# First two layers: mixed tiles turned inside the last input unit, and the gate's Silu split

## What is computed

```python
proj = jnp.einsum('btd,de->bte', x, w_in[l])                 # 2048 -> 7168 columns
ca, cg, hq, hf, hi, hg, rq, rk, rv, rg = jnp.split(proj, split_idx, axis=-1)
y_conv = conv_mixer(ca, cg, ...)                             # 512 columns
y_hgrn = hgrn2_mixer(hq, hf, hi, hg, ...)                    # 768 columns
y_ret = retention_mixer(rq, rk, rv, rg, positions, ...)      # 768 columns
mix = jnp.concatenate([y_conv, y_hgrn, y_ret], axis=-1)
h = jnp.einsum('bte,ed->btd', mix, w_out[l])
x = layer_norm(ALPHA * x + h, ln1_g[l], ln1_b[l])
...                                                          # feed-forward, layer norm
```

```python
o = ((o - mu) * lax.rsqrt(var + LN_EPS)).reshape(b, t, D_RET) * gn_g + gn_b
return jax.nn.silu(g_in) * o                                 # g_in is rg, the last 768 columns of proj
```

## Time and profile before

| | us |
|---|---|
| time, median of 3 runs | 3481.93 (3479.95 to 3484.95) |
| time of the profiled execution | 3486.19 |
| span of the profiled execution, first to last instruction | 3484.4 |
| mean granted TensorE clock | 0.992 of full |

### The profile page before, as it was taken

One profiled execution on the slowest core, in us unless ns is written; L12 is line 12 of the kernel. 1 busy time (PEld: TensorE's weight loads), 2 busy tenths in 40 slices (PEclk: granted clock), 3 DMA queues, 4 the chain that ended last, 5 costly groups with the idle time before them and its releaser, 6 DMA issues.

```text
span 3484.4 us, 42756 instructions
## 1 busy us (share of the span) xinstructions
PE 3397.1 (97%) x15987; PEld 2831.8 (81%) x15987; DVE 2222.3 (64%) x2582; ACT 1586.0 (46%) x1958; POOL 352.4 (10%) x390
## 2 busy tenths in 40 slices
PE   8999999999999999989999999999999989999999
PEld 7788778888888787878788888888888879888877
DVE  6986566555555788855665656666446676655654
ACT  4544444444444446434444434344455643455553
POOL 0034001010101000340101010100000132000100
PEclk9999999999999999999999999999999999999999
DMA  7645566666666664446766676766655601565634
GB/s 238 181 140 163 181 199 219 200 211 200 212 199 212 190 194 151 145 151 193 245 210 208 203 207 203 207 196 208 186 178 176 205 6 56 188 189 169 179 118 163
DMA packets 333659, 633.83 MB, mean 182 GB/s; under 512 B 27545, under 2 KB 37785, under 8 KB 331819
## 3 DMA queue, kind: packets, MB, share of 16 engines
q1 hardware_dynamic: 313104, 595.93, 55.4%
q0 software_dynamic: 11168, 29.18, 2.7%
q10 hardware_dynamic: 9216, 6.30, 0.6%
HBM read 612.44 MB, written 2.10 MB: 176 GB/s over the span
## 4 chain that ended last, share of the span: by engine, by line
PE 85%; DVE 9%; ACT 3%; DMA 1%; POOL 1%; issue 1%; SPq 0%; DVEq 0%; ACTq 0%; POOLq 0%
PE ps_unit L279 26%; PE ps_unit L281 26%; PE ps_unit L280 26%; DVE sb_w_lo L262 3%; DVE sb_conv_y L1260 2%; PE ps_mix L2732 2%; PE ps_mix L1334 1%; DMA sb_raw<-in_w_in_dram 1%; ACT sb_w_hi L255 1%; PE ps_mix L708 0%; PE ps_mix L307 0%; DVE sb_x L438 0%; PE ps_mix L3129 0%; PE ps_mix L3109 0%; DMA sb_raw<-in_e_w_in_dram 0%
## 5 line engine op out<-in xcount | busy, mean ns | idle before, releaser
L262 DVE TENSOR_TENSOR sb_w_lo<-sb_raw,sb_w_hi 128x1024 fp32r<-128x1024 f32 x1120 | 1377.2, 1245 | 1001.4 <-ACT sb_w_hi L255 996.4
L255 ACT ACTIVATE sb_w_hi<-sb_raw 128x1024 fp32r<-128x1024 f32 x1120 | 1172.6, 1059 | 1456.9 <-DMA sb_raw<-in_w_ff_dram 532.3
L279 PE MATMUL ps_unit<-sb_w_hi,sb_a_hi 128*128 128x512 f32 x3456 | 1365.3, 395 | 16.0 <-DVE sb_a_lo L750 11.1
L281 PE MATMUL ps_unit<-sb_w_hi,sb_a_lo 128*128 128x512 f32 x3456 | 1351.6, 391 | 0.0
L280 PE MATMUL ps_unit<-sb_w_lo,sb_a_hi 128*128 128x512 f32 x3456 | 1350.7, 391 | 0.0
L279 PEld LDWEIGHTS ps_unit<-sb_w_hi,sb_a_hi 128*128 128x128 f32 x3456 | 652.8, 189 | 155.2 <-DVE sb_a_lo L750 12.7
L281 PEld LDWEIGHTS ps_unit<-sb_w_hi,sb_a_lo 128*128 128x128 f32 x3456 | 652.0, 189 | 137.6
L280 PEld LDWEIGHTS ps_unit<-sb_w_lo,sb_a_hi 128*128 128x128 f32 x3456 | 653.1, 189 | 132.2
L279 PE MATMUL ps_unit<-sb_w_hi,sb_f_hi 128*128 128x512 f32 x1024 | 399.3, 390 | 0.0
L281 PE MATMUL ps_unit<-sb_w_hi,sb_f_lo 128*128 128x512 f32 x1024 | 398.6, 389 | 0.0
L280 PE MATMUL ps_unit<-sb_w_lo,sb_f_hi 128*128 128x512 f32 x1024 | 398.5, 389 | 0.0
(11 more groups left out here) (463 smaller groups left out, 1975.6 us busy)
## 6 DMA issues: line engine op xcount, KB each, us to landing
sb_raw<-in_w_ff_dram SPq DMA_DIRECT2D x512, 512.0 KB, 3.8
sb_raw<-in_w_in_dram SPq DMA_DIRECT2D x224, 512.0 KB, 3.6
...
```

The source lines that it names most:

```text
L255: k.nc.scalar.activation(k.w_hi[:, j], k.raw[:, j], ACT.Copy).then_inc(k.hi_ready, 1)
L262: k.nc.vector.tensor_tensor(k.w_lo[:, j], k.raw[:, j], k.w_hi[:, j].bitcast(F32), ALU.subtract).then_inc(k.lo_ready, 1)
L279: k.nc.tensor.matmul(acc, hi[:, kt, tokens], w_hi, start=kt == 0, stop=False)
L281: last = k.nc.tensor.matmul(acc, lo[:, kt, tokens], w_hi, start=False, stop=kt == KT - 1)
```

## The change

It moves the turning of all eight banks in each of the two layers, four of them into the last input unit.

- Retention's output stands ahead of block 89 in layer 0 and of block 91 in layer 1 (`RET_OUT`).
- Banks 0, 1 and 2 are transposed right behind it, and bank 3 ahead of block 92 (layer 0) or 94 (layer 1). ScalarE's rounding of them waits for the block of the last input unit that still reads that part of `a_hi`. Banks 1 and 2 lie in half 0 of `ps_unit`, banks 0, 3 and 4 in bank 3 of `ps`, and banks 5, 6 and 7 in banks 0 to 2 of `ps`.
- Bank 4 is turned ahead of block 2 of the out product, and 5, 6 and 7 ahead of block 4.
- `turn_source`'s first 5 are raised at the start of `dve_retention`.
- The gate's Silu goes in two: the first 256 columns in `proj` during the last unit, the other 512 straight from the sums in `ps_unit`, in the place of the last unit's copy. VectorE's gate products wait for that and stand ahead of its last three weight blocks.

```diff
 def pe_out_units(pe, k, mixed, tile):
     first = k.block0["pe"]
     k.block0["pe"] += OUT_UNITS * BLOCKS
-    pe_turn_start(pe, k, mixed)
     for c in range((OUT_UNITS - 1) * BLOCKS):
-        if c < BLOCKS:
-            pe_turn_step(pe, k, mixed, c)
+        if c == 0:
+            pe.wait_ge(*k.turn_lo.next("pe", 3))
+        if c == 2:
+            pe.wait_ge(*k.turn_lo.next("pe bank", 3))
+            pe_mixed_bank(pe, k, mixed, 4)
+        if c == 4:
+            for g in (5, 6, 7):
+                pe_mixed_bank(pe, k, mixed, g)
+        if 3 <= c < BLOCKS:
+            pe.wait_ge(*k.turn_lo.next("pe"))
         pe_block(pe, k, first, c, k.a_hi, k.a_lo)
+def mixed_bank(k, g):
+    return k.ps_unit[:, 0, g - 1, :] if g in (1, 2) else k.ps[:, 3 if g in (0, 3, 4) else g - 5, :]
+def pe_mixed_bank(pe, k, mixed, g):
+    pe.wait_ge(*k.turn_source.next("pe"))
+    pe_turn_bank(pe, k, mixed, g, mixed_bank(k, g))
+def act_mixed_bank(act, k, run, g):
+    act.wait_ge(k.block_done, run.first + run.blocks + g + 1)
+    act_turn_bank(act, k, g, mixed_bank(k, g))
...
 # pe_retention
-    upto(run, 88 + LATE * l)
+    upto(run, RET_OUT[l])
...
     last.then_inc(*k.r_o.up())
+    for g in (0, 1, 2):
+        pe_mixed_bank(pe, k, first_mix_tile(k), g)
+    upto(run, RET_OUT[l] + 3)
+    pe.wait_ge(*k.turn_lo.next("pe bank"))
+    pe_mixed_bank(pe, k, first_mix_tile(k), 3)
     run.rest()
+RET_OUT = (89, 91)
 # act_retention
-    upto(run, 91 + LATE * l)
+    upto(run, RET_OUT[l] + 1)
+    for g in (0, 1, 2):
+        act_mixed_bank(act, k, run, g)
     act.wait_ge(*k.r_var.next("act"))
     a.activation(k.r_rstd[:], k.r_mv[:, :, 1], ACT.Sqrt, ...)
+    run(1)
+    act.wait_ge(*run.evacuated(run.blocks // BLOCKS - 1))
+    rg = k.proj[:, :, RG:RG_LAST]
+    a.activation(rg, rg, ACT.Silu).then_inc(*k.r_gate.up())
+    upto(run, RET_OUT[l] + 4)
+    act_mixed_bank(act, k, run, 3)
     run.rest()
-    rg = k.proj[:, :, RG:RG + HW]
-    act.wait_ge(*run.evacuated(run.blocks // BLOCKS))
-    a.activation(rg, rg, ACT.Silu).then_inc(*k.r_gate.up())
+def act_take_first(act, k):
+    take_proj = act_take_proj(act, k, HQ)
+    def take(b0, s, i):
+        if HQ + (2 * i + s) * NC < RG_LAST:
+            return take_proj(b0, s, i)
+        wait_unit(act, k, b0, s)
+        k.nc.scalar.activation(k.proj[:, :, RG_LAST:RG_LAST + NC], k.ps_unit[:, s], ACT.Silu).then_inc(k.evacuated, BLOCKS)
+    return take
 # dve_retention: turn_source moved to its start; then, behind the statistics of o
-    upto(run, 92 + LATE * l)
+    for g in (0, 1, 2):
+        dve_turn_bank(dve, k, g, mixed_bank(k, g))
+    run(1)
...
-    upto(run, 94 + LATE * l)
+    run(1)
+    dve_turn_bank(dve, k, 3, mixed_bank(k, 3))
     step(v.tensor_tensor(y, y, k.r_shift[:]..., ALU.add))
-    run.rest()
     dve.wait_ge(*k.r_gate.next("dve"))
+    dve.wait_ge(*run.evacuated(run.blocks // BLOCKS))
     for p in range(HEADS // 2):
         v.tensor_tensor(y, y, gate, ALU.mult).then_inc(*k.turn_source.up())
+    run.rest()
+    dve_turn_bank(dve, k, 4, mixed_bank(k, 4))
...
-                act_out_units(act, k, act_ln_root(act, k))
+                act_out_units(act, k, act_ln_root(act, k), late={AHEAD + 1: (4,), AHEAD + 3: (5, 6, 7)})
-                dve_out_units(dve, k, LayerNorm(ALPHA))
+                dve_out_units(dve, k, LayerNorm(ALPHA), late={AHEAD + 2: (5, 6, 7)})
```

More of the change, by code:

```diff
@@ L497, in pe_out_units @@
     k.block0["pe"] += OUT_UNITS * BLOCKS
-    pe_turn_start(pe, k, mixed)
     for c in range((OUT_UNITS - 1) * BLOCKS):
-        if c < BLOCKS:
-            pe_turn_step(pe, k, mixed, c)
+        if c == 0:
[8 more added lines that the diff above has]
+            pe.wait_ge(*k.turn_lo.next("pe"))
         pe_block(pe, k, first, c, k.a_hi, k.a_lo)
+    k.turn_lo.next("pe bank", 4)
     pe_seam_last(pe, k, first, OUT_UNITS - 1, k.a_hi, k.a_lo, tile)
@@ L536, in pe_pair_after_seam, with act_out_units @@
         pe_block(pe, k, first, c, k.a_hi, k.a_lo)
-def act_out_units(act, k, root):
+def mixed_bank(k, g):
[6 more added lines that the diff above has]
+    act_turn_bank(act, k, g, mixed_bank(k, g))
+def act_out_units(act, k, root, late={}):
     first = k.block0["act"]
@@ L543, in act_out_units, with dve_out_units @@
         act_split(act, k, first, c)
+        for g in late.get(c, ()):
+            act_turn_bank(act, k, g, mixed_bank(k, g))
     act_seam(act, k, first, OUT_UNITS * BLOCKS, root)
-def dve_out_units(dve, k, norm):
+def dve_out_units(dve, k, norm, late={}):
     first = k.block0["dve"]
@@ L555, in dve_out_units @@
             dve_split(dve, k, first, u * BLOCKS + c)
+            for g in late.get(u * BLOCKS + c, ()):
+                dve_turn_bank(dve, k, g, mixed_bank(k, g))
     last = OUT_UNITS - 1
@@ L1036 @@
 RQ, RK, RV, RG = (2 * CONV_C + (4 + n) * HW for n in range(4))
+RG_LAST = RG + HW - NC
 LEVELS = 7
@@ L1683, in dve_retention @@
     v.memset(k.r_rstd[:], 0.0).then_inc(*k.r_rope_free.up())
+    dve.wait_ge(*k.conv_done.next("dve"))
+    dve.sem_inc(*k.turn_source.up(BLOCKS - HEADS // 2))
     upto(run, 85 + LATE * l)
@@ L1692, in dve_retention @@
             .then_inc(*k.r_kept.up())
-    upto(run, 89 + LATE * l)
+    upto(run, RET_OUT[l] + 1)
     dve.wait_ge(*k.r_o.next("dve"))
@@ L1706, in dve_retention @@
     for t in range(TT):
+        if t:
+            run(1)
         for h in range(HEADS):
@@ L1711, in dve_retention @@
     step(last)
-    dve.wait_ge(*k.conv_done.next("dve"))
-    dve.sem_inc(*k.turn_source.up(BLOCKS - HEADS // 2))
     y = k.proj[:, :, RQ:RQ + HW]
     step(v.tensor_tensor(y, y, k.r_gain[:].unsqueeze(1).to_broadcast([P, TT, HW]), ALU.mult))
-    upto(run, 94 + LATE * l)
+    run(1)
+    dve_turn_bank(dve, k, 3, mixed_bank(k, 3))
     step(v.tensor_tensor(y, y, k.r_shift[:].unsqueeze(1).to_broadcast([P, TT, HW]), ALU.add))
-    run.rest()
     dve.wait_ge(*k.r_gate.next("dve"))
+    dve.wait_ge(*run.evacuated(run.blocks // BLOCKS))
     for p in range(HEADS // 2):
```

5 lines of the change are left out of this document (2 added, 3 removed).

## The result

The changed kernel takes 3463.43 us (median of 5 runs, 3457.69 to 3465.19), the kernel before beside it 3479.95 us (median of 5). The ratio is 0.9944 with the interval [0.9933, 0.9956]: 19.5 us of 3481.93, between 15.3 and 23.3. The forecast was 3464.4 us, between 3460.5 and 3471.5. The profiled execution took 3463.43 us with a span of 3461.6.

The account below looks back on a forecast made before the run. TensorE, busy 97% of the span, was taken as the bound, so time comes only from its waits and slow clock. 7.60 plus 10.48 us removed, 18.1, less 0.6 added gave 17.5: 3481.93 to 3464.4 us, range 3460.5 to 3471.5.

Parts of the forecast that it names:

- All the waits named: TensorE idle to be removed: 4.75 and 1.26 us in layer 0, 4.97 and 2.50 us in layer 1.
- the new one of 0.6 us: Layer 1: the output, one block earlier, waits 0.6 us for the last masked score; the clock was assumed to stay.
- The three terms: Layer 0: 4.75 us idle before the out product, 1.59 slow block behind it, 1.26 ahead of retention's output; together 7.60.
- the removed part: Layer 1, 10.48 us: idle 4.97 and 2.50, slow transposes 1.76, slow block behind them 1.25.
- the term left out of the sum: Layer 1: slow clock in the next four transposes, 0.97 us against 0.60, kept only for the low end.
- weight block 99: Layer 0: its low part, behind the gate products, ready at 385.5 and needed at 389.9, 4.4 us to spare.
- 1.6 us, from one row, for any new stall: Slow clock behind any new wait, taken from layer 0's block of 4.44 us in place of 2.85.
- The prediction's own use of the rule, 5.5 us: Both layers: half of 4.0, 3.7 and some 3.3 us as throttling penalty, 5.5 us where the rows give 4.6.
- A new stall: Rival: bank 5's round or weight block 99 late, 7.2 us come back, gain 10.3, 3471.6 us; chance 0.13.
- the weights: Rival: TensorE reaches the out product sooner but waits for weights, gain about 4 us, 3478; chance 0.04.
- the late load: Rival: weight block 101 lands late, delaying gate products and weight block 99; 7 us slower, 3489; chance 0.03.
- The fall of the clock: Rival: clock falls anyway with 12 transposes behind retention's output, 1.6 us per layer, gain 14.3, 3467.6 us; chance 0.08.

Follow-up runs that it names:

- e12_out88: Changed kernel with retention's output at its old places in both layers, behind block 87 in layer 0 and 91 in layer 1: 3459.00 us, ratio 0.9940.
- e9_out92: Changed kernel with layer 1's retention output moved one block later: 3459.31 us, ratio 0.9943.
- The dose: Changed kernel with eight extra ScalarE copies ahead of the Silu on the sums in layers 0 and 1: 3471.11 us, ratio 0.9977.
- e1 to e4: Change in layer 0 only, 0.9974; layer 1 only, 0.9972; kernel before with Silu's split only, 0.9986; changed kernel, banks 0 to 3 turned behind input again, 0.9987.
- e5_no_split: Changed kernel with the gate's Silu in one piece as before: 3457.93 us, ratio 0.9931.

## Where the prediction was right, and the step that was wrong

**Direction and size.** 3464.4 us was forecast, a gain of 17.5, and 3463.43 was measured, inside 3460.5 to 3471.5; the ratio gives 19.5 [15.3, 23.3] and the stretches 18.5. All the waits named were gone, the new one of 0.6 us came where it was said, and the clock held in both stretches. The mechanism was right. The sum was 1.0 us short of the stretches, and what follows says in which terms.

**The step that was wrong: the price of a wait.** The sum took each wait at the idle time of its row. By the distance between starts a wait holds TensorE longer than that; one reason is that the idle time counts only from the modelled end of the last matmul. e12_out88 puts the 1.26 us ahead of the output back and loses 1.50. Taking the new wait of 0.55 us away (e9_out92) gives 0.83. In layer 1 of before, 7.86 us lie between the starts of the last input block (1556.91) and of the transposes (1564.77); less a block of 2.72 that is 5.14, for an idle time of 4.97. And the 32 transposes of the eight banks, without their idle time, held TensorE for 3.41 us in layer 0 of before (1.91 of them in the group of 16 with the idle time behind it) and for 3.16 in the changed kernel, where no wait follows any of them: 0.25. So each wait costs 0.17 to 0.28 us on top of its idle time, and the prediction put that at nothing.

**Layer 0, 7.60 forecast, 8.11 measured.** The three terms are right in kind. The missing 0.51 is that price, once ahead of the output (0.24) and once behind the 16 transposes (0.25).

**Layer 1, 10.48 less 0.6 forecast, 10.42 measured.** Of the removed part 0.77 was missing: the price twice (0.17 and, as in layer 0, about 0.25), and the term left out of the sum, bank 4's transposes, which take 0.60 us now in place of 0.97, 0.37. The new wait cost 0.83 in place of 0.6.

**Room.** On TensorE every block and transpose laid out along the clock of before came within 0.4 us. With 1.4 us between the clocks: gate products end at 385.9 (384.3 forecast), weight block 99 ready at 387.0 for 391.12, 4.1 to spare for 4.4; bank 5 ready at 395.8 for 397.9, 2.1 for 2.3; bank 3's transposes wait for 365.8 and stand at 371.12, 5.3 for 5.5. The dose gives 4.2 for the first by itself. Silu on the sums took 1.01 us, as the copy does. Two items were off by 0.8 us: VectorE's shift ended earlier (382.1 for 381.5), and ScalarE's split of weight block 105 later (394.16 for 391.9). Its load was there 5.2 us behind the block that frees its slot (387.92 to 393.10), where one row had given 4.0. ScalarE was free only 0.3 us ahead of bank 5's transposed values; a load later by more than that would have used up part of the 2.1 us.

**Slow clock behind a wait.** The other price that was off, and it didn't decide here: I took 1.6 us, from one row, for any new stall. Behind eight waits of 2.5 to 4.8 us (before, e1 to e4) the next block took 4.10 to 5.29 us, and 5.26 behind the one of the dose. The price is 1.2 to 2.5 us, and it goes with how much of the block ran at the lower level: the granted clock over the block was 0.67 for 4.10 us, 0.62 for 4.44, 0.53 for 5.07 and 0.50 for 5.26. By the rule of the Trainium skill, "TensorE: Matmul & The Clock Gate", "Terms", the penalty is about the throttled time multiplied by one minus the granted ratio: an estimate of 2.6 us for the 5.26 at 0.50. This case's trace agrees (2.5). The prediction's own use of the rule, 5.5 us, took stretches for throttled that were so only in part: with the granted clocks 0.57, 0.50 and 0.67 of 4.0, 3.7 and 4.1 us the estimate is 4.9, and the rows gave 4.6.

**The rivals.** A new stall, the weights and the late load show in no row of either stretch. The fall of the clock behind 12 transposes did not come in any of the 11 executions that have them inside a unit in one layer or both. The Trainium skill, same page, "Part 4: PE-mode transpose", by which transposes don't engage the full clock, is not borne out by this case's trace: the 8 transposes of banks 1 and 2 took 1.04 us in the middle of a stretch at 1.00 (356 to 372 us). A long stretch of transposes alone stands in no run here.

**What the prediction did not ask** is which part of the change does the work. It took the split as a part of the whole, at no cost and no gain of its own; e5_no_split shows that it is worth nothing beside the early turn. The numbers to see it were there: 4.4 us to spare, and the split saves 2.8.
